# Weighted values of an attention head in rounded and low parts: a change to a decoder-layer kernel on one Trainium2 core

## The reference

```python
s_s = einsum('bgrqd,bgqkd->bgrqk', qb, k_g);  p_s = masked_softmax(s_s - slopes * d_s, d_s >= 0)
o_s = einsum('bgrqk,bgqkd->bgrqd', p_s, v_g)          # selected branch; o_w the same with k_w, v_w
o_c = einsum('bgrqc,bgcd->bgrqd', p_c, vc)            # 31 compressed blocks
return gb[..., 0:1] * o_c + gb[..., 1:2] * o_s + gb[..., 2:3] * o_w
```

## Time and profile before

| | |
|---|---|
| median of 3 runs | 1409.69 us (1409.45 to 1410.24) |
| the profiled execution | 1411.29 us, span 1409.6 us |
| PE busy | 1341.8 us (95%) |
| weight loads (PEld) | 1055.9 us (75%) |
| DVE busy | 792.1 us (56%) |
| ACT busy | 622.6 us (44%) |
| mean granted clock of TensorE | 0.985 of full speed |
| the four groups | from about 113 to 780 us of the span |

### The profile page before, as it was taken

One profiled execution on the slowest core, in us unless ns is written; L12 is line 12 of the kernel. 1 busy time (PEld: TensorE's weight loads), 2 busy tenths in 40 slices (PEclk: granted clock), 3 DMA queues, 4 the chain that ended last, 5 costly groups with the idle time before them and its releaser, 6 DMA issues.

```text
span 1409.6 us, 16678 instructions
## 1 busy us (share of the span) xinstructions
PE 1341.8 (95%) x6333; PEld 1055.9 (75%) x6333; DVE 792.1 (56%) x1505; ACT 622.6 (44%) x1105; POOL 4.1 (0%) x19
## 2 busy tenths in 40 slices
PE   3998999999998999989999999999979999999999
PEld 2787777777676777777767888887768888888887
DVE  3427855777467774768656343333356666665222
ACT  5524565455654546454655443222353333333120
POOL 1000000000000000000000000000000000000000
PEclk9998999999999999999999999999989999999999
DMA  7311212212112122121211833333313333333231
GB/s 244 78 47 30 61 53 53 76 30 68 46 37 80 41 58 63 31 75 45 68 53 60 270 103 89 92 96 132 116 45 90 90 101 94 90 92 118 97 120 68
DMA packets 185588, 116.28 MB, mean 82 GB/s; under 512 B 25917, under 2 KB 169637, under 8 KB 185509
## 3 DMA queue, kind: packets, MB, share of 16 engines
q1 hardware_dynamic: 182053, 108.92, 26.8%
q10 hardware_dynamic: 3456, 6.29, 1.2%
HBM read 106.80 MB, written 8.39 MB: 82 GB/s over the span
## 4 chain that ended last, share of the span: by engine, by line
PE 82%; DVE 10%; ACT 5%; issue 2%; SPq 1%; DMA 0%; ACTq 0%; DVEq 0%
PE g L478 18%; PE g L479 17%; PE g L480 17%; PE ob L674 5%; PE t L471 5%; PE s L630 3%; PE s L784 1%; PE s L783 1%; PE s L782 1%; PE s L609 1%; PE t L537 1%; DVE piece_e L1485 1%; PE g L784 1%; PE t L784 1%; PE g L783 1%
## 5 line engine op out<-in xcount | busy, mean ns | idle before, releaser
L1198 DVE TENSOR_TENSOR wlo<-wraw,whi 128x1024 fp32r<-128x1024 f32 x175 | 213.7, 1222 | 207.8 <-ACT whi L816 207.6
L478 PE MATMUL g<-hT_hi,whi 128*128 128x512 f32 x616 | 264.9, 430 | 4.8 <-DVE hT_lo L1205 4.2
L479 PE MATMUL g<-hT_lo,whi 128*128 128x512 f32 x616 | 246.3, 400 | 0.0
L480 PE MATMUL g<-hT_hi,wlo 128*128 128x512 f32 x616 | 246.0, 399 | 0.0
L816 ACT ACTIVATE whi<-wraw 128x1024 fp32r<-128x1024 f32 x175 | 184.4, 1054 | 120.0 <-PE g L784 46.6
L478 PE MATMUL g<-h2T_hi,whi 128*128 128x512 f32 x352 | 141.2, 401 | 3.6 <-DVE h2T_lo L1205 3.6
L478 PEld LDWEIGHTS g<-hT_hi,whi 128*128 128x128 f32 x616 | 118.2, 192 | 29.9 <-issue 5.9
L479 PE MATMUL g<-h2T_lo,whi 128*128 128x512 f32 x352 | 140.2, 398 | 0.0
L480 PE MATMUL g<-h2T_hi,wlo 128*128 128x512 f32 x352 | 140.0, 398 | 0.0
L480 PEld LDWEIGHTS g<-hT_hi,wlo 128*128 128x128 f32 x616 | 117.4, 191 | 28.4
L479 PEld LDWEIGHTS g<-hT_lo,whi 128*128 128x128 f32 x616 | 118.3, 192 | 21.4 <-issue 1.9
(11 more groups left out here) (287 smaller groups left out, 2114.1 us busy)
## 6 DMA issues: line engine op xcount, KB each, us to landing
wraw<-in_w_in SPq DMA_DIRECT2D x152, 256.0 KB, 3.3
wraw<-in_ffn_w_up SPq DMA_DIRECT2D x88, 256.0 KB, 3.3
wraw<-in_ffn_w_down SPq DMA_DIRECT2D x44, 256.0 KB, 3.2
wraw<-in_w_proj_b SPq DMA_DIRECT2D x32, 256.0 KB, 3.3
yT_lo<-spill SPq DMA_DIRECT2D x6, 1024.0 KB, 8.1
spill<-zchan ACTq DMA_DIRECT2D x16, 256.0 KB, 2.0
wraw<-in_w_proj_a SPq DMA_DIRECT2D x16, 256.0 KB, 3.3
wraw<-in_w_out SPq DMA_DIRECT2D x16, 256.0 KB, 3.5
```

Of the source, the lines that this page charges most:

```text
L478: nc.tensor.matmul(gb[par][:, :], w, hi, start=k == 0, stop=False)
L479: nc.tensor.matmul(gb[par][:, :], w, lo, start=False, stop=False)
L480: return nc.tensor.matmul(gb[par][:, :], wl, hi, start=False, stop=last)
L1198: V.tensor_tensor(wlo[u % SLOTS][:, :, :], wraw[u % 2][:, :, :], whi[u % SLOTS][:, :, :].bitcast(F32), ALU.subtract).then_inc(w_lo, 1)
```

## The change

The weighted values become fp32r products. ACT rounds the values of both branches into `vst` once per group, DVE writes their low part beside it: 64 rounded and 64 low columns make 128 stationary columns. The transposed probabilities are split as well: ACT copies them rounded into `pT[0]`, DVE subtracts the copy from the PSUM bank into `pT[1]` and only then releases the bank. Each tile is multiplied in two passes, `pT[0]` and `pT[1]`, with the same stationary tile. So one head fills the whole bank `ob`, high and low values in its two halves; ACT copies one half into `obuf` and DVE adds the other (`out_half`, `out_fold`). The compressed branch is done per head in the same form.

The stage of unit n is moved behind the first k-tile of the next unit's GEMM, the last one behind the first k-tile of block BF. Other work changes its engine: the head tiles' float32 copy goes (DVE multiplies the gain itself, from the bank), the bias of a head and the scaling of the 512-wide tile go to ACT, the first tap of the convolution is a second evacuation on ACT, and DVE takes the state product from PSUM (`from_state`). The causal mask is folded into `negdist`.

```diff
-        vcg = sb("vcg", [P, R, DH], c=ph1)
+        vcg = sb("vcg", [P, R, 2, DH], F32R, ph1)
+        vst = sb("vst", [P, 2, NT, 2, DH], F32R, ph1)
...
-        obuf = [sb(f"obuf{i}", [P, T], c=ph1) for i in range(2)]
+        obuf = hstage
...
-        piece_d = sb("piece_d", [P, 3 * T], c=ph1)
+        pT = [sb(f"pT_{n}", [P, WID], F32R, ph1) for n in ("hi", "lo")]
+        pcT = [sb(f"pcT_{n}", [P, T], F32R, ph1) for n in ("hi", "lo")]
...
+                def weighted_values(n):
+
+                    r, br = n // 2, n % 2
+                    if n == 0:
+                        pe.wait_ge(v_lo, g * 2 + 2)
+                    if br == 0:
+                        pe.wait_ge(o_fold, g * R + r)
+                    for j in range(NT):
+                        pe.wait_ge(t_rel, g * TG + (TP + K_UNIT[n] + j + 1))
+                        w = P * (NT - j)
+                        for part in pT:
+                            ins = nc.tensor.matmul(ob[:, P * j:T], vst[:, br, j, :, :].rearrange("p a d -> p (a d)"),
+                                                   part[:, offT[j]:offT[j] + w],
+                                                   start=br == 0 and j == 0 and part is pT[0], stop=False)
+                    if br:
+                        pe.wait_ge(t_rel, g * TG + (TP + K_CMP + 2))
+                        for part in pcT:
+                            ins = nc.tensor.matmul(ob[:, :], vcg[:, r, :, :].rearrange("p a d -> p (a d)"), part[:, :],
+                                                   start=False, stop=part is pcT[1])
+                    ins.then_inc(pv_done, 1)
...
-                        pe.wait_ge(p_ready, g * 8 + (n + 1))
+                        pe.wait_ge(p_ready, g * 16 + (2 * n + 2))
...
+                    if n:
+                        between[1] = lambda: weighted_values(n - 1)
...
-                    orow = ob[DH * (r % 2):DH * (r % 2) + DH, :]
-                    if n == 4:
-                        pe.wait_ge(y_ready, g * 6 + 1)
-                    for j in range(NT):
-                        pe.wait_ge(t_rel, g * TG + (TP + K_UNIT[n] + j + 1))
-                        w = P * (NT - j)
-                        ins = nc.tensor.matmul(orow[:, P * j:T], tok[:, 2 + br, j, DH:P], pT[:, offT[j]:offT[j] + w],
-                                               start=br == 0 and j == 0, stop=False)
-                    if n == 3:
-                        pe.wait_ge(t_rel, g * TG + (TP + K_CMP + 2))
-                    if n % 4 == 3:
-                        ins = nc.tensor.matmul(ob[:, :], vcg[:, r - 1:r + 1, :].rearrange("p r d -> p (r d)"), pcT[:, :],
-                                               start=False, stop=True)
-                    ins.then_inc(pv_done, 1)
...
+                grp_gemm(BF, {1: lambda: weighted_values(7), 4: lambda: xz_transposes(0), 5: lambda: xz_transposes(1),
...
-                    nc.scalar.activation(xraw[q % 2][:, :], src[:, :], ACT.Copy).then_inc(g_rel, 1)
+                    nc.scalar.activation(xraw[q % 2][:, :], src[:, :], ACT.Copy)
+                    col = g * 4 + q if q < 4 else g + (16 if q == 4 else 20)
+                    nc.scalar.activation(xc[:, q, :], src[:, :], ACT.Identity, scale=pcol[:, 0, col + 72 + CW:col + 73 + CW],
+                                         bias=pcol[:, 0, col + CB_:col + CB_ + 1]).then_inc(g_rel, 1)
...
+                def head_bias(r):
+
+                    nc.scalar.activation(hbias[r % 2][:, :], negdist[:, :], ACT.Copy,
+                                         scale=slopes[:, g * R + r:g * R + r + 1]).then_inc(hb_ready, 1)
+
                 for b in range(4):
                     evac_tok(b)
+                head_bias(0)
                 evac_x(BX)
+                head_bias(1)
...
-                    act.wait_ge(r_lo, g * 6 + (e + 1))
-                    nc.scalar.activation(full[e % 2][:, :], tb[par][:, :], ACT.Copy, scale=pcol[:, 0, gain:gain + 1]).then_inc(r_full, 1)
                     dst = (qs[0], khh[0], khh[1], *qs[1:])[e]
-                    nc.scalar.activation(dst[:, :], tb[par][:, :], ACT.Copy, scale=pcol[:, 0, gain:gain + 1]).then_inc(t_rel, 1)
+                    nc.scalar.activation(dst[:, :], tb[par][:, :], ACT.Copy, scale=pcol[:, 0, gain:gain + 1]).then_inc(r_hi, 1)
                     if e == 3:
                         evac_x(BX + 1)
-
...
+                for br in range(2):
+                    nc.scalar.activation(vst[:, br, :, 0, :], tok[:, 2 + br, :, DH:P], ACT.Copy).then_inc(v_hi, 1)
...
+                def out_half(r):
+
+                    act.wait_ge(pv_done, g * 8 + (2 * r + 2))
+                    if r % 2 == 0:
+                        act.wait_ge(o_stored[r // 2], g * 16 + 16)
+                    to, fr = DH * (r % 2), DH * (1 - r % 2)
+                    nc.scalar.activation(obuf[r // 2][to:to + DH, :], ob[fr:fr + DH, :], ACT.Copy).then_inc(o_half, 1)
...
+                def scale_tile(n):
+
+                    act.wait_ge(ps_ready, g * 8 + (n + 1))
+                    pr = prob[n % 2][:, 0:T]
+                    nc.scalar.activation(pr, pr, ACT.Copy, scale=pscale[n % 2][:, 3:4]).then_inc(p_ready, 1)
...
                 exps(0)
+                scale_tile(0)
...
                 for n in range(8):
-                    if n == 4:
+                    if n in (2, 4, 6):
+                        out_half(n // 2 - 1)
+                    if n == 5:
                         o_out(0)
+                    if n % 2 == 0 and 0 < n < 6:
+                        head_bias(n // 2 + 1)
                     for j in range(NT):
                         tau, par = T_(K_UNIT[n] + j)
                         w = P * (NT - j)
                         t_wait(tau)
                         if n > 0 and j == 0:
                             act.wait_ge(pv_done, g * 8 + n)
-                        nc.scalar.activation(pT[:, offT[j]:offT[j] + w], tb[par][:, 0:w], ACT.Copy).then_inc(t_rel, 1)
+                        nc.scalar.activation(pT[0][:, offT[j]:offT[j] + w], tb[par][:, 0:w], ACT.Copy).then_inc(pT_hi, 1)
...
                     if n < 7:
                         exps(n + 1)
                     b = BX + 2 + n
                     (evac_x if b < BZ else evac_z)(b)
+                    if n < 7:
+                        scale_tile(n + 1)
                     if n == 5:
                         act.wait_ge(conv_done, g * 6 + 6)
...
                     x_, y_ = xraw[q % 2], xc[:, q, :]
                     dve.wait_ge(g_rel, g * GROUP_BLOCKS + (B_GRP + BX + q + 1))
-                    seq.done(V.tensor_scalar(y_, x_[:, :], w[3], pcol[:, 0, ds(col + CB_, 1)], ALU.mult, ALU.add))
                     for s in range(1, 4):
-                        seq.fence()
+                        if s > 1:
+                            seq.fence()
                         ins_ = V.scalar_tensor_tensor(y_[:, s:T], x_[:, 0:T - s], w[3 - s], y_[:, s:T], ALU.mult, ALU.add)
...
                 def head_lo(e):
 
-                    dve.wait_ge(r_full, g * 6 + (e + 1))
-                    rel(K_BACK + e)
+                    dve.wait_ge(r_hi, g * 6 + (e + 1))
+                    bank_, gain = tb[(TP + K_BACK + e) % 2], HEADS[e][2]
                     if e in (1, 2):
-                        V.tensor_tensor(kll[e - 1][:, :], full[e % 2][:, :], khh[e - 1][:, :].bitcast(F32),
-                                        ALU.subtract).then_inc(r_lo, 1)
+                        V.scalar_tensor_tensor(kll[e - 1][:, :], bank_[:, :], pcol[:, 0, gain:gain + 1],
+                                               khh[e - 1][:, :].bitcast(F32), ALU.mult, ALU.subtract).then_inc(r_lo, 1)
                     else:
                         low = qs[max(e - 2, 0)][DH:P, :]
-                        V.tensor_tensor(low, full[e % 2][DH:P, :], low.bitcast(F32), ALU.subtract).then_inc(r_lo, 1)
+                        V.scalar_tensor_tensor(low, bank_[DH:P, :], pcol[DH:P, 0, gain:gain + 1], low.bitcast(F32),
+                                               ALU.mult, ALU.subtract).then_inc(r_lo, 1)
+                    dve.wait_ge(r_lo, g * 6 + (e + 3))
+                    dve.sem_inc(t_rel, 1)
...
-                    seq.done(V.tensor_tensor(pscale[n % 2][:, :], pscale[n % 2][:, :], gcols[:, :, r, 1 + br], ALU.mult))
-                    seq.fence()
-                    for i in range(NT):
+                    V.tensor_tensor(pscale[n % 2][:, :], pscale[n % 2][:, :], gcols[:, :, r, 1 + br],
+                                    ALU.mult).then_inc(ps_ready, 1)
+                    dve.wait_ge(ps_ready, g * 8 + (n + 1))
+                    for i in range(NT - 1):
                         pr = prob[n % 2][:, off[i]:off[i] + P * (i + 1)]
                         ins_ = V.tensor_scalar(pr, pr, pscale[n % 2][:, i:i + 1], None, ALU.mult)
-                        if i < NT - 1:
+                        if i < NT - 2:
                             seq.done(ins_)
                     ins_.then_inc(p_ready, 1)
 
```

(37 more changed lines are left out.)

80 lines of the change are left out of this document (39 added, 41 removed).

## The result

| | before | after |
|---|---|---|
| median | 1409.62 us (4 runs, 1409.45 to 1410.24) | 1440.61 us (4 runs, 1438.77 to 1441.35) |
| profiled span | 1409.6 us | 1438.8 us |
| granted clock, mean | 0.985 | 0.975 |

The ratio is 1.022, 95% interval 1.020 to 1.0235: slower by 31 us. The forecast was 1431 us with a range to 1446. The time lies in the range and on the forecast's side, 10 us above its value and 5 us above the 1420 to 1435 that the forecast gave as its own; by the time alone the clock rival (1439) is nearer.

What follows compares the result with a forecast made beforehand. PE bounds the kernel now, but its saving was to be lost in waits on DVE and ACT: 3.1 (units and behind) + 1.75 (head) + 0.5 (scan) = 5.3 us per group, 21 in all, giving 1431 us; range 1408 to 1446.

Steps and rivals of the forecast that it cites:

- the clock rival: Granted clock falls in each group's head as PE idles, costing 1.4 to 2.8 us per group: 1439 us; chance 0.20.
- The circle: Convolution, evacuations, rounding, scaling, transposes, differences, weights' low part, next convolution: 10.6 us against PE's 9.3, so PE waits 1.3.
- The stage: Weighted values on PE, eight fp32r matmuls shaped like the score stage: 1.25 us instead of 2.30.
- unit 6: Scaling ahead of the SiLU waits for DVE's reciprocal; copy, difference and second transposes follow late: +2.6 us.
- unit 7: PE waits 1.5 us for the weights' low part behind the last differences, no score stage covering it: -0.3 us net.
- Unit 0: Weighted-values stage gone, but third tile's transposes wait for copy and difference, next weights behind: -1.1 us.
- The head: Third head tile's transposes wait on DVE behind the weights' low part, the fifth tile's wait goes: net +1.75 us per group.
- the stretch behind unit 7: Last stage and compressed product inside GEMM BF, +1.6 us; scan-stage products waiting for DVE, +0.5 per group.
- The rival's other row: Granted clock 0.50 from 1025 to 1028 us, read as following a PE standstill of 3 us; evidence for the clock's fall.
- Faster: Rival: ACT and DVE get round in 9.3 us instead of 10.6, PE keeps its gain: 1378 at best, half way 1394; chance 0.12.
- A dear fp32r product: Rival: fp32r with these operands costs what fp32 did, PE's own unit 10.3 us: 1441 us; chance 0.04.
- None alone turns the sign: Cheaper differences, scaling, second evacuation, SiLU or hops each still leave a loss per group; together below -3 possible.

Runs made afterwards that it cites:

- The products of zeros: Five 512-column fp32r products of zeros added behind each unit's weighted values: changed kernel 1454.06 us (+13.5), changed kernel with the four queue moves 1420.41 us (+25.9).
- the run with 12 products: Changed kernel plus 12 unread 512-column fp32r products per group on PE ahead of the third head tile's transposes: 1435.25 us (-5.4).
- the run with the head's move: Changed kernel with the low part of unit 0's weights on DVE behind the first three head tiles' low parts, not ahead: 1430.13 us (-10.5).
- the run with scaling and SiLU: Changed kernel with ACT's 512-wide scaling ahead of the next weights' rounding and the SiLU one unit later: 1421.60 us.
- four moves: Changed kernel with unit 0's weights' low part later, SiLU one unit later, scaling before rounding, weights' low part before the last differences: 1394.52 us.
- the SiLU's move: Changed kernel with the SiLU over the convolved channels one unit later on ACT, behind the last head's scaling: 1429.31 us (-11.3).

## Why the prediction was right

**The mechanism.** The circle was forecast at 10.6 us and measured 10.71; its parts 2.89 (end of convolution to transposes: 348.90 - 345.85 = 3.05), 2.87 (first to second transposes: 2.92). PE's wait was forecast at 1.3 and was 1.27 in unit 3 (0.97 and 0.79 in units 2 and 4). The stage was forecast at 1.25 and took 1.21. Six of eight units came within 0.12 us of the forecast's difference; unit 6 cost 0.45 more and unit 7 0.6 more. Unit 0's agreement is partly luck: in two groups it came out 1.6 us above the forecast. The products of zeros show it as a cause, not only as a pattern.

**The head.** Forecast +1.75; the wait cost 1.74 in the second group (the head's +3.31 less the 1.57 of the clock, by the run with 12 products). The term that was mis-sized is the clock: the sum put it at nothing, a rival carried it at 0.20, and it came true beside the forecast's waits and not instead of them, 1.57 us in the head, and in unit 6, which no case had named. The rival's time, 1439, was in fact the nearer one; the forecast is right by its waits and its way, not by its last digits. Of the 10 us between forecast and time, the groups hold 7.9 if the second stands for all (1.97 each): the head +1.56, units 6 and 7 +1.06, the small ones together -0.3, the stretch behind unit 7 -0.34. In unit 6 two k-tiles of 1.32 and 1.28 us stand where 0.70 is usual, which is 1.2 us by these rows. Less of it reached the time: in the run with the head's move three groups have the same wait of 2.18 us without slow k-tiles, and their units 6 and 7 take 21.61 us together against 22.25, so the dip was worth 0.64. The remaining 1.7 is the 1.6 us that the forecast took off because the profiled execution of before ran above its median; that of the changed kernel (1440.53 us) did not. The account closes so well only with the second group for all: the others lost 6.75, 7.63 and some 9.2 us, and 1.7 us was gained ahead of the first head, which the forecast had at nothing.

**The argument against the clock** was that waits of 1.05 and 1.23 us in that head cost nothing. It was read from shorter waits than the one forecast. The wait of 1.99 us left by the head's move cost no k-tile either; the one of 3.13 did in the second to fourth group of the changed kernel, and so did that of 2.18 in unit 6. But length alone doesn't decide: the 2.18 us cost nothing in three groups of the run with the head's move, and in the run with scaling and SiLU the fourth group's wait of 3.12 us was followed by k-tiles of 0.7 us. The rival's other row was misread: ahead of 1025 us PE had stood for 5.48 us and not for 3.

**The rivals.** Faster: the circle didn't close in PE's period; in units 3 to 5 it could be made to, by order alone, as four moves showed. A dear fp32r product: refuted, 1.21 us a stage. "None alone turns the sign" was said of the prices of instructions and held, but not of their order, which the prediction took as given: moving one 1.14 us instruction gave 28 us, which alone left 3 of the 31 us of loss.

## What to carry to other kernels

When work is taken from the engine that bounds a stage and put on two that have room, add up not the busy times but the closed circle of waits; if it is longer than the new period, the gain turns into a wait of just that length. Then look for an instruction in that circle that could stand in one of its idle gaps: here one of 1.14 us, moved ahead of 0.62 us of other work, was worth 28 us (in the last unit, ahead of 1.78 us). Try each repair in the old kernel too, and look at the whole group: the SiLU's move also saved two table loads per group, in both kernels. And test whether an engine is the bound by giving it more work: what costs nothing was no bound.

## What the runs showed of the hardware

- A standstill of PE of 3.13 us was followed by k-tiles at 1.43 us instead of 0.70, and twelve useless products in it took that away: 5.4 us gained by more work. Not every such wait was: one of 3.12 us in another run had k-tiles of 0.7 behind it.
- Groups with the same instructions differ by up to 3.5 us within one trace, and waits and gains per group have to be compared group by group. A slow stretch taken away in one place came back in part in another (1.5 us behind the scan after the head's move).
- 32 matmuls with 32 columns in a row (3.7 to 5.2 us) were followed by matmuls at the lower clock in every group of the kernel before, the changed one and that of four moves (k-tiles of up to 1.43 us); 8 at a time between k-tiles, they left the mean granted clock at 0.98 in the second group, but not in the first (0.63 from 128 to 138 us).
- ACT loaded a table (1.28 us) four times per group with the SiLU between exponentials, and twice with it behind the last ones.
- The second evacuation with scale and bias took 0.78 us against 0.60 for the plain copy of the same 128x512 bank (0.66 and 0.50 start to start).
